# Stick-breaking heads by pairs: the score products of two heads alternate between the row halves of the matrix engine

## The reference, cut to what matters

```python
def stick_breaking_attention(q, k, v):
    scale = HEAD_DIM ** -0.5
    ...
        z = jnp.einsum('bhqd,bhkd->bhqk', qb, kb).astype(jnp.float32) * scale
        mask = s[None, :] < t[:, None]
        log_1m = jnp.where(mask, jax.nn.log_sigmoid(-z), 0.0)
        between = lax.cumsum(log_1m, axis=3, reverse=True) - log_1m
        w = jnp.where(mask, jnp.exp(jax.nn.log_sigmoid(z) + between), 0.0)
        outs.append(jnp.einsum('bhqk,bhkd->bhqd', w.astype(vb.dtype), vb))

def hybrid_layer(x, pos, norm_g, w_in, ...):
    h = rms_norm(x, norm_g)
    proj = h @ w_in
    ...
    o_a = stick_breaking_attention(split_heads(sb_q, SB_HEADS), split_heads(sb_k, SB_HEADS),
                                   split_heads(sb_v, SB_HEADS))
    y_a = merge_heads(o_a) * jax.nn.silu(sb_z)
    ...
    merged = jax.nn.sigmoid(gate_a) * (y_a @ w_up_a) + jax.nn.sigmoid(gate_b) * (y_b @ w_up_b)
```

## Time and profile before

| what | value |
|---|---|
| runs | 3011.9 to 3020.4 us, median 3014.6 |
| profiled execution | 3014.1 us, span 3012.4 us |
| TensorE busy | 2741.5 us (91% of the span) |
| VectorE, ScalarE, GpSimd busy | 1807.3, 654.2, 627.2 us |
| mean granted TensorE clock | 0.955 of full speed |
| chain that ended last | TensorE 66%, DMA 22%, VectorE 8% |
| stick-breaking stage, layer L = 0 | 2058.4 to 2159.9 us, 101.5 us |
| stick-breaking stage, layer L = 1 | 2641.2 to 2735.9 us, 94.8 us |

### The profile page before, as it was taken

One profiled execution on the slowest core, in us unless ns is written; L12 is line 12 of the kernel. 1 busy time (PEld: TensorE's weight loads), 2 busy tenths in 40 slices (PEclk: granted clock), 3 DMA queues, 4 the chain that ended last, 5 costly groups with the idle time before them and its releaser, 6 DMA issues.

```text
span 3012.4 us, 47854 instructions
## 1 busy us (share of the span) xinstructions
PE 2741.5 (91%) x18359; PEld 1707.0 (57%) x18360; DVE 1807.3 (60%) x3159; ACT 654.2 (22%) x1329; POOL 627.2 (21%) x612
## 2 busy tenths in 40 slices
PE   7997999999998878788788889999899999998998
PEld 3444444677864434444334444766568877755687
DVE  3557599527656666666666666853464558246544
ACT  3118102102120000000000001323353113144420
POOL 1006012324420000000000003120165441204642
PEclk9999999999999999999989889999899999999999
DMA  8347222234438999999999995311002223200030
GB/s 230 114 157 262 84 71 69 78 109 149 145 114 351 427 426 426 426 426 427 426 427 426 427 426 227 127 56 56 1 2 104 90 74 114 84 28 1 32 109 28
DMA packets 126423, 584.19 MB, mean 194 GB/s; under 512 B 8756, under 2 KB 27796, under 8 KB 92516
## 3 DMA queue, kind: packets, MB, share of 16 engines
q1 hardware_dynamic: 124064, 581.58, 48.7%
q0 software_dynamic: 480, 0.39, 0.7%
q10 hardware_dynamic: 1764, 0.66, 0.1%
HBM read 580.34 MB, written 2.27 MB: 193 GB/s over the span
## 4 chain that ended last, share of the span: by engine, by line
PE 66%; DMA 22%; DVE 8%; issue 2%; ACT 1%; SPq 0%; DVEq 0%; ACTq 0%
PE PS L2316 32%; PE PS L2061 24%; DMA S<-in_w 21%; PE PS L1087 8%; PE PS L1364 1%; DVE TAIL L1795 1%; DVE RSTD L1748 1%; SPq L381 0%; DVE S L1838 0%; DVE tri L2955 0%; DMA ring<-decay_rows 0%; DVE TAIL L1806 0%; DVE S L3130 0%; DVE TAIL L3004 0%; DMA S<-in_x 0%
## 5 line engine op out<-in xcount | busy, mean ns | idle before, releaser
L2316 PE MATMUL PS<-nT,ring 128*128 128x512 f32 x1248 | 547.4, 596 | 4.0 <-DMA ring<-in_w_in 2.5
L759 DVE SCALAR_TENSOR_TENSOR xT<-PS,MOD,xT 128x512 f32<-128x512 f32 x520 | 359.3, 744 | 70.1 <-PE PS L2316 70.1
L2316 PEld LDWEIGHTS PS<-nT,ring 128*128 128x128 f32 x1248 | 235.3, 191 | 288.4 <-issue 281.6
L2316 PE MATMUL PS<-TAIL 128*32 128x256 f32 (+2 forms) x3216 | 308.7, 468 | 42.8 <-ACT TAIL L602 37.7
L2316 PE MATMUL PS<-S,TAIL 128*32 128x256 f32 x3072 | 214.9, 434 | 56.6 <-DMA S<-in_w 50.9
L2316 PEld LDWEIGHTS PS<-TAIL 128*32 128x32 f32 (+2 forms) x3216 | 135.1, 136 | 190.9 <-issue 87.2
L2316 PE MATMUL PS<-ring,TAIL 128*32 128x256 f32 (+1 forms) x2304 | 180.7, 463 | 62.2 <-DMA ring<-in_w 49.7
L1020 POOL TENSOR_SCALAR nT<-xT,AD 128x512 f32<-128x512 f32 x4 | 6.2, 1565 | 969.4 <-DVE xT L759 969.4
L2316 PEld LDWEIGHTS PS<-S,TAIL 128*32 128x32 f32 x3072 | 117.2, 121 | 154.6 <-issue 115.3
L2316 PEld LDWEIGHTS PS<-ring,TAIL 128*32 128x32 f32 (+1 forms) x2304 | 99.7, 130 | 153.2 <-issue 124.9
L2119 DVE TENSOR_TENSOR TAIL<-PAIR,PS 128x256 f32<-128x256 f32 x46 | 19.4, 421 | 265.9 <-PE PS L2061 265.8
(11 more groups left out here) (491 smaller groups left out, 4385.1 us busy)
## 6 DMA issues: line engine op xcount, KB each, us to landing
S<-in_w SPq DMA_DIRECT2D x96, 2048.0 KB, 22.4
ring<-in_w SPq DMA_DIRECT2D x65, 2048.0 KB, 20.0
ring<-in_w_in SPq DMA_DIRECT2D x40, 2048.0 KB, 7.9
nT<-in_w SPq DMA_DIRECT2D x31, 2048.0 KB, 23.1
ring<-in_w_ada SPq DMA_DIRECT2D x12, 2048.0 KB, 10.2
TAIL<-decay_rows SPq DMA_DIRECT2D x20, 640.0 KB, 5.4
ring<-in_w_ssm_out SPq DMA_DIRECT2D x4, 2048.0 KB, 8.2
ring<-in_cmp_w SPq DMA_DIRECT2D x4, 2048.0 KB, 8.3
```

What stands on the lines that cost most here:

```text
L759: dve.scalar_tensor_tensor(out=xT[:, c, :], in0=PS[:, bank, :], scalar=MOD[:, 40 + c:41 + c], in1=xT[:, c, :], op0=ALU.mult, op1=ALU.add). ...
L2316: return pe.matmul(o, l, r, start=start, stop=stop)
```

## The change

The score products of a pair of heads are issued together, each product of head 2c followed by the same of head 2c+1. TensorE's order is then, by pairs c: scores(c), for c > 0 the outputs of pair c-1, half a gate chunk (for c = 0 a whole one, 8 products), sums(2c), sums(2c+1), and for c < 3 half a gate chunk. The scores of a pair wait for the weights of both heads of the pair before. ScalarE does soft of both heads and then weights of both, VectorE `ya` of the pair before, then softplus of both and diag of both. No instruction is added or taken away; semaphores are counted to the pair's values.

```diff
-                def z_scores(h):
-                    c, p0, b = h // 2, 64 * (h % 2), 1536 * (h % 2)
-                    if h >= 2:
-                        pe.wait_ge(S("off_w"), SBH * L + h - 1)
-                        pe.wait_ge(S("diag_w"), SBH * L + h - 1)
-                    elif h == 0:
+                def z_scores(c):
+
+                    if c:
+                        pe.wait_ge(S("off_w"), SBH * L + 2 * c)
+                        pe.wait_ge(S("diag_w"), SBH * L + 2 * c)
+                    else:
                         pe.wait_ge(S("pj_evac"), PJL * L + PJL)
-                    else:
                         pe.wait_ge(S("kcd_ready"), L + 1)
-                    k_, q_ = SBK[p0:p0 + 64, c, :], SBQ[p0:p0 + 64, c, :]
-                    for j in range(NT):
-                        m = acc(PS2[:, b + P * j:b + P * j + P], k_[:, P * j:P * j + P], q_[:, P * j:P * j + P], j == 0)
-                    for j in (0, 2, 1):
-                        m = acc(PS2[:, b + OFF[j]:b + OFF[j] + OFFW[j]], k_[:, P * j:P * j + P], q_[:, P * (j + 1):T],
-                                j in (0, 1))
-                    m.then_inc(S("z_ready"), 1)
+                    for j, off in [(j, False) for j in range(NT)] + [(j, True) for j in (0, 2, 1)]:
+                        for e in range(2):
+                            p_, b = slice(64 * e, 64 * e + 64), 1536 * e
+                            if off:
+                                m = acc(PS2[:, b + OFF[j]:b + OFF[j] + OFFW[j]], SBK[p_, c, P * j:P * j + P],
+                                        SBQ[p_, c, P * (j + 1):T], j in (0, 1))
+                            else:
+                                m = acc(PS2[:, b + P * j:b + P * j + P], SBK[p_, c, P * j:P * j + P],
+                                        SBQ[p_, c, P * j:P * j + P], j == 0)
+                            if off and j == 1:
+                                m.then_inc(S("z_ready"), 1)
...
-                def gate_early(h):
-
-                    for i in range(8 if h == 0 else 4 if h < SBH - 1 else 0):
-                        at = i if h == 0 else 4 * h + 4 + i
+                def gate_early(first, n_):
+
+                    for at in range(first, first + n_):
                         n, k = at // KD, at % KD
...
-                z_scores(0)
-                for h in range(SBH):
-                    if h + 1 < SBH:
-                        z_scores(h + 1)
-                    gate_early(h)
-                    z_sums(h)
-                    if h >= 2 and h % 2 == 0:
-                        sb_out(h // 2 - 1)
+                for c in range(SBH // 2):
+                    z_scores(c)
+                    if c:
+                        sb_out(c - 1)
+                        gate_early(KD * c + KD // 2, KD // 2)
+                    else:
+                        gate_early(0, KD)
+                    z_sums(2 * c)
+                    z_sums(2 * c + 1)
+                    if c + 1 < EARLY:
+                        gate_early(KD * (c + 1), KD // 2)
                 sb_out(SBH // 2 - 1)
...
-                    act.wait_ge(S("z_ready"), SBH * L + h + 1)
+                    act.wait_ge(S("z_ready"), SBH * L + 2 * (h // 2) + 2)
...
-                soft(0)
-                for h in range(SBH):
-                    if h + 1 < SBH:
-                        soft(h + 1)
+                for h in range(0, SBH, 2):
+                    soft(h)
+                    soft(h + 1)
                     weights(h)
+                    weights(h + 1)
...
-                softplus(0)
-                for h in range(SBH):
-                    if h + 1 < SBH:
-                        softplus(h + 1)
-                    diag(h)
-                    if h % 2 == 0 and h >= 2:
-                        ya(h // 2 - 1)
+                for c in range(SBH // 2):
+                    if c:
+                        ya(c - 1)
+                    softplus(2 * c)
+                    softplus(2 * c + 1)
+                    diag(2 * c)
+                    diag(2 * c + 1)
                 ya(SBH // 2 - 1)
```

## The result

The changed kernel takes 2977.7 us (median of 4 runs, 2975.2 to 2980.9), the kernel before 3013.2 us (4 runs, 3011.7 to 3020.4). The ratio is 0.9883, 95% interval 0.9863 to 0.9903: faster, by 35.5 us. The forecast was 2988, the range 2981 to 2997. The direction was right and the size outside the range.

A forecast was written before the change was run, and what follows sets the result against it. TensorE, busy 91% of the span, was taken as the bound. Savings of 10.9 us per layer, 21.7 for two, plus 4.3 from the clock made 26.0 off 3014.1: forecast 2988 us, range 2981 to 2997.

The forecast's parts named there:

- A pair of scores costs 2.39 us: Score products of two heads, alternating on the array's row halves, run side by side: 2.39 us where 4.78 stood.
- the prediction's bound for it, 4.5: Upper bound for a pair's score products if nothing runs side by side: 4.5 us.
- The overlap of the narrow weight loads: Weight loads of the 128-column score passes on different row halves overlap, read from four loads starting within 0.1 us.
- Rivals 1 and 2: Products overlap but narrow loads do not, 2996.6 us, chance 0.08; halves do not run side by side, 3009 us, chance 0.04.
- Waits ahead of the scores go: TensorE's waits for the `off_w` exponential ahead of the scores of heads 2, 3, 5, 7 vanish: 4 x 0.97 us.
- Waits ahead of the sums come: New TensorE waits for VectorE's mask products ahead of a pair's sums: 0.39 us even head, 0.17 us odd head.
- The round: A round of two heads in the stick-breaking stage takes 19.46 us against 22.26, 2.80 less.
- each head's sums were priced at 3.57 us: Price of one head's sums on TensorE at the full clock, 2.15 + 1.42 = 3.57 us.
- The sum of a layer at the full clock, 10.9 us: Saving per stick-breaking stage: first pair 1.5, wait ahead of head 2 0.97, three rounds of 2.80, together 10.9 us.
- The clock: Half-clock stretches in both stages shrink or go, giving 0 to 8.5 us; the middle, 4.3 us, was taken.
- rival 3: Row-half work itself makes the clock fall after every pair, so the kernel gets slower: 3022 us, chance 0.03.
- rival 4: All low-clock stretches go, giving 8.5 us in place of 4.3: 2984 us, chance 0.13.

The follow-up runs named there:

- experiment 1: Changed kernel with each pair's 14 score products in single-head order, new order otherwise kept; 2999.4 us, ratio to the kernel before 0.9947.
- experiment 4: Changed kernel with a round's eight gate products divided 5 ahead of the pair's sums and 3 behind, instead of 4 and 4; 2976.1 us, ratio 0.9862.
- experiment 2: Kernel before, in its old order, with only the scores of heads 0 and 1 alternating between row halves; 3004.8 us, ratio 0.9956.
- experiment 3: Changed kernel with only the first pair of each layer in single-head order, the rest alternating; 2990.7 us, ratio to the kernel before 0.9918.
- 11: Single repeat execution of the changed kernel with only each layer's first pair in single-head order, for its clock; 2986.8 us.
- experiment 8: Changed kernel with every pair's block of 14 alternating score products issued twice; 2998.3 us, ratio to the kernel before 0.9957.
- experiment 5: The changed kernel run again with no edit, for a second look at the clock; 2979.2 us, ratio to the kernel before 0.9897.
- 6: Changed kernel with gate products divided anew, two of them in the idle time ahead of the last outputs; 2967.5 us, ratio 0.9856.
- 12: Single repeat execution of the changed kernel with gate products divided anew and two ahead of the last outputs; 2980.2 us.

## Why the prediction was right and wrong

*A pair of scores costs 2.39 us: right.* After: 2.39 to 2.40 in every round. It rested on the units' two products side by side, and experiment 1 shows the other case in the same kernel, 4.03 (the prediction's bound for it, 4.5, was too high). The overlap of the narrow weight loads, read from four records, held for 20 passes of 128 columns a pair: the 28 loads of a block start two by two. Rivals 1 and 2 are dead.

*Waits ahead of the scores go: right. Waits ahead of the sums come: right in place, a little small.* 0.79 us a round (experiment 4) against 0.56. The round still came out within 0.06 us of the forecast, 19.52 against 19.46, because a second miss stands against this one: each head's sums were priced at 3.57 us and take 3.47 to 3.48 where nothing waits (experiment 4). That closeness is partly luck.

*The sum of a layer at the full clock, 10.9 us: right.* In the second layer the stage lost 14.38 us, and 6.9 us at half clock are 3.4 of them: 10.9 remain. In the first it lost 21.1; the low stretches there were 10.3 at the start, twice 3.4 and 3.4 at the last output product, 20.5 us or 10.2 lost, and 10.9 remain.

*The clock: wrong, and this is the step that failed.* It read: "At most that gives 2 x 1.7 in the middle, 1.7 at the end, and 1.7 per layer at the start if the clock rises 3.4 us sooner: 8.5 us", and 4.3 was taken. The two stages gave back 13.6 us (10.2 + 3.4). The middle and the end came as in the bound. At the starts I only let the low stretch be shorter, as if its beginning were given by the idle time ahead, which the change leaves. It never began: 0 of 16 against 10 of 12. The bound should have been the whole of the earlier trace rows, 5.1 and 3.4 us at the starts, 13.6 in all. Nothing in the rows excluded that, and the prediction itself said that idle time and half-filled rows stood together before each fall. The prediction had most of it in its own text: rival 3 counts 11.9 us lost in both stages (it leaves out the last outputs' 1.7), while rival 4, "all low-clock stretches go", is priced at 8.5. With 21.7 + 13.6 the forecast would have been 2979, 1.1 us from the measured 2977.7. What the runs show in place of the bound: the starts' falls depend on how the first pair's scores are issued. Alternating them in the old order takes the falls away (experiment 2), and putting them back in single order in the new one brings them back (3 of 4 starts in experiments 3 and 11).

The end was less sure than the bound made it look: with alternating scores throughout (experiments 4 and 8) the last outputs still ran at half clock in three of four stages. That the changed kernel's profiled executions (after, and experiment 5) show none there is not explained by the change.

The remaining 1.1 us of the profiled difference (1.9 behind the stages, less 0.9 ahead of them) were not forecast and are about as large as what changes between two profiles of one kernel.

*Rival 3, the clock that answers the other way:* dead. The added block of alternating scores in experiment 8 did not bring the clock down at the starts either. Its price also misread the rows: the clock did not fall "after 28 passes on row halves" but 1.1 us behind the start of the block (2058.42, the low stretch from 2059.50 on the earlier trace rows).

## What to carry to other kernels

Products that fill 64 of the 128 rows cost about what full ones cost (0.213 us for 128 columns here, a gate product of 128 rows 0.22). Where a second set lies in the other 64 partitions and, as here, goes to other PSUM banks, issue the two alternately, product by product: the second came free (2.39 us for one head, 2.39 for two). When a change fills rows or idle time, read every low stretch of the granted clock in the stage and let the bound take in all of it, its beginning too. When waits move from one place to another, divide the filling work by the length of each wait, down to the single product.

## What the runs showed of the hardware

- Two alternating products of 64 rows on the two halves start 0.007 us apart, and their weight loads too (after).
- Two consecutive single-head blocks overlap at their joint: a pair costs 4.03 us (experiment 1) and not 2 x 2.39 = 4.78, with no alternation in the program; the records of both heads start together for half a microsecond in the middle. In the first profile too, 28 records took less than twice 14.
- At the starts and in the rounds the clock fell only where idle time and work on half the rows came together (behind the last sums, at 2.2 us of idle time, it fell in some profiles of either kind). Idle time of 1.5 us with alternating scores: 0 of 16. Half the rows with no idle time: 0 of 18 pairs. Both: 10 of 12 at the starts, 7 of 24 behind the shorter waits in the old rounds. Why the others held is open.
- The low stretch behind a stage changes from kernel to kernel without any edit there. With the idle time ahead of the last outputs filled (6, 12) it was 17.1 us and not 6.8, in four of four stages; but it was 17.1 behind both stages of experiment 3 too, where nothing was filled, and 13.7 behind the first of experiment 4. What ties them was not tested, and in medians it adds or hides up to 4 us per layer.
